# First attention of a two-layer fp32 step: two heads' scores inside the last query chunk, the query sums in two parts, one rope on GpSimd

## What is computed

```python
qa, ka, va, qi, ki, wi, cqlat, ckv, kr = split_cols(u @ w_in, AB_SPLITS)
q  = rope(rmsnorm(qa.reshape(nb, t, 8, 128), g_aq), pos)          # mixer A: 8 heads
...
qb = (rmsnorm(cqlat, g_qlat) @ w_uq).reshape(nb, t, 8, 128 + 64)  # mixer B
qn = rmsnorm(qb[..., :128], g_qn)
qr = rope(rmsnorm(qb[..., 128:], g_qr), pos)
...
# mixer A: scores, a mask from an index (top-k), softmax, values
s = einsum('bqcgd,bqscd->bqcgs', qg, k_sel) * 128 ** -0.5
p = softmax(where(valid, s, -inf)); o = einsum('bqcgs,bqscd->bqcgd', p, v_sel)
# mixer B: the same with nope and rope parts and other keys
```

## Time and profile before

| | |
|---|---|
| time, median of 3 runs | 2862.4 us (2862.0 to 2863.89) |
| the profiled execution | 2863.7 us, its span 2861.7 us |
| PE busy | 99% of the span, DVE 50%, ACT 37%, POOL 7% |
| the chain that ended last | PE 97%, DVE 2%, ACT 1% |
| the first attention with its query chunks | about 241 to 317 us of the span |
| mean granted TensorE clock | 0.999 of 2.4 GHz |

### The profile page before, as it was taken

One profiled execution on the slowest core, in us unless ns is written; L12 is line 12 of the kernel. 1 busy time (PEld: TensorE's weight loads), 2 busy tenths in 40 slices (PEclk: granted clock), 3 DMA queues, 4 the chain that ended last, 5 costly groups with the idle time before them and its releaser, 6 DMA issues.

```text
span 2861.7 us, 45023 instructions
## 1 busy us (share of the span) xinstructions
PE 2843.7 (99%) x18666; PEld 2798.6 (98%) x18666; DVE 1428.0 (50%) x1546; ACT 1069.6 (37%) x1236; POOL 186.0 (7%) x112
## 2 busy tenths in 40 slices
PE   9999999999999999999999999999999999999999
PEld 9997799999999999999999999899999999999999
DVE  7677645543443344344466774546444443444443
ACT  5334533332332333233335633434333332432332
POOL 2000002000000000000221241112000000000000
PEclk9999999999999999999999999999999999999999
DMA  6433024444444444444444444244444444444443
GB/s 232 139 114 111 30 89 143 144 140 145 143 140 148 140 145 142 141 146 140 145 149 155 154 146 148 97 160 149 148 152 151 148 152 149 148 152 149 149 153 135
DMA packets 112783, 405.25 MB, mean 142 GB/s; under 512 B 12656, under 2 KB 14752, under 8 KB 112480
## 3 DMA queue, kind: packets, MB, share of 16 engines
q1 hardware_dynamic: 108864, 392.64, 41.2%
q0 software_dynamic: 1616, 6.31, 0.6%
q10 hardware_dynamic: 2128, 3.66, 0.3%
HBM read 396.48 MB, written 6.09 MB: 141 GB/s over the span
## 4 chain that ended last, share of the span: by engine, by line
PE 97%; DVE 2%; ACT 1%; issue 0%; DMA 0%; ACTq 0%; DVEq 0%
PE PS L1426 31%; PE PS L1430 30%; PE PS L1431 30%; PE PS L1505 0%; ACT pr L498 0%; DVE pr L925 0%; DVE w_lo L858 0%; PE PS L1706 0%; DVE rb L1067 0%; PE PS L1503 0%; PE PS L1881 0%; PE PS L1489 0%; ACT w_hi L450 0%; PE PS L1753 0%; PE PS L1752 0%
## 5 line engine op out<-in xcount | busy, mean ns | idle before, releaser
L858 DVE TENSOR_TENSOR w_lo<-stage,w_hi 128x1024 fp32r<-128x1024 f32 x734 | 919.6, 1255 | 1192.6 <-ACT w_hi L450 1192.2
L450 ACT ACTIVATE w_hi<-stage 128x1024 fp32r<-128x1024 f32 x740 | 784.0, 1060 | 1628.2 <-PE PS L1431 1618.7
L1426 PE MATMUL PS<-xh,w_hi 128*128 128x336 f32 (+1 forms) x3264 | 1021.5, 313 | 1.1 <-DVE kk L1102 0.6
L1430 PE MATMUL PS<-xl,w_hi 128*128 128x336 f32 (+1 forms) x3248 | 1015.3, 313 | 0.0
L1431 PE MATMUL PS<-xh,w_lo 128*128 128x336 f32 (+1 forms) x3248 | 1014.6, 312 | 0.0
L1426 PE MATMUL PS<-hh,w_hi 128*128 128x336 f32 (+1 forms) x2032 | 635.2, 313 | 0.0
L1431 PE MATMUL PS<-hh,w_lo 128*128 128x336 f32 (+1 forms) x2032 | 635.1, 313 | 0.0
L1430 PE MATMUL PS<-hl,w_hi 128*128 128x336 f32 (+1 forms) x2032 | 634.9, 312 | 0.0
L1426 PEld LDWEIGHTS PS<-xh,w_hi 128*128 128x128 f32 x3264 | 614.4, 188 | 3.9 <-DVE w_hi L848 1.1
L1431 PEld LDWEIGHTS PS<-xh,w_lo 128*128 128x128 f32 x3248 | 612.1, 188 | 0.0
L1430 PEld LDWEIGHTS PS<-xl,w_hi 128*128 128x128 f32 x3248 | 611.5, 188 | 0.4
(11 more groups left out here) (343 smaller groups left out, 1527.7 us busy)
## 6 DMA issues: line engine op xcount, KB each, us to landing
stage<-in_wstream SPq DMA_DIRECT2D x740, 512.0 KB, 3.3
out_s<-so POOLq DMA_DIRECT2D x8, 256.0 KB, 2.6
x<-in_x_in SPq DMA_DIRECT2D x6, 336.0 KB, 7.2
out_y<-x ACTq DMA_DIRECT2D x3, 672.0 KB, 4.0
dmask<-in_ret POOLq DMA_DIRECT2D x4, 352.0 KB, 6.1
stage<-in_wstream SPq DMA_DIRECT2D x4, 256.0 KB, 3.6
s<-in_s_in POOLq DMA_DIRECT2D x1, 1024.0 KB, 5.3
x<-in_x_in SPq DMA_DIRECT2D x4, 168.0 KB, 3.7
```

The source lines that it names most:

```text
L450: act.activation(w_hi[s], halves_of(s), ACT.Copy).then_inc(hi_ready, 1)
L858: dve.tensor_tensor(w_lo[s], halves_of(s), w_hi[s].bitcast(F32), ALU.subtract).then_inc(lo_ready, 1)
L1426: pe.matmul(out, wh, rh, start=first, stop=False)
L1430: pe.matmul(out, wh, rl, start=False, stop=False)
```

## The change

Five edits, all between the last chunks of the query projection and the end of the first attention:

- The scores of heads 0 and 1 move from the head of `attend` into the last query chunk on PE (before its first and before its second unit), with their minima on DVE (`minima`) and their exponentials on ACT (`exponentials`). They use banks 2, 3 and 0, 1. `attend` begins at step 2, and its banks alternate the other way round.
- `query_sums` is split. The four matmuls of the rope parts (`pair_sums`) run after the first unit of the second chunk, into bank 2; the eight others run at step 3, not 1, into bank 7. Each part has its own DVE copy to `sdq`.
- The rope of mixer B's queries goes from DVE to POOL: five `tensor_tensor` instructions over 1344 elements per partition, with a new tile `rbq` in the place of `rb4`, begun when `pair_sums` is done (the tile lies where the squares were).
- `latl`, `gqk`, the memset of `ptb` and the norm of head 0 are placed between the minima of heads 0 and 1 and the last copy of the queries on DVE.
- The split of unit `U_KN` + 3 (the second value unit) moves behind the first attention on ACT and DVE.

```diff
+TURNS = 5
+        rbq = place("rbq", [P, 4, T], A + 28 * TB)
 # ACT
             for k in range(6):
-                split(U_UQ + 4 + k)
+                if k < 5:
+                    split(U_UQ + 4 + k)
                 ab_piece(7, 4 + k)
+                if k >= 4:
+                    exponentials(k - 4)
...
-            attend(0, 0, 0)
+            attend(0, 0, 0, 2)
+            split(U_KN + 3)
             split(U_KN + 4)
 # DVE
+            def minima(g, h, bias, scale, b0):
+                dve.wait_ge(sc_psum, g + 1)
+                if g >= 3:
+                    dve.wait_ge(pt_psum, g - 2)
+                ...                       # the three reductions that stood in attend
+            def normed(g):
+                ...                       # reciprocal and three products, as in attend
-                    if g0 == 0 and s == 1:
-                        dve.wait_ge(qb_ms, 1)
-                        dve.tensor_copy(sdq[0:8], PS[0:8, 4:6, 0:T]).then_inc(qb_taken, 1)
+                    if g0 == 0 and s == 3:
+                        dve.wait_ge(qb_ms, 2)
+                        dve.tensor_copy(sdq[0:8, 0], PS[0:8, 7, 0:T]).then_inc(qb_taken, 1)
...
-                if (g, j) == (7, 7):
-                    dve.wait_ge(qa_turned, 2)
-                    half_sines(rb4, qr, 2, 0, "qr")
-                    half_sines(rb4, qr, 2, 1, "qr")
-                if (g, j) == (7, 8): ...  # product with gain and cosines
-                if (g, j) == (7, 9): ...  # sum, qb_turned
...
             for k in range(6):
+                if k == 4:
+                    dve.wait_ge(bias_ready, 1)
+                    dve.wait_ge(qa_rinv, 2)
+                    minima(0, 0, biasA, scale_a, 2)
+                    dve.wait_ge(lath_ready, 2)
+                    dve.tensor_tensor(latl[:], lat[:], lath[:].bitcast(F32), ALU.subtract).then_inc(latl_ready, 1)
+                    dve.tensor_tensor(gqk[:], gcol("qn"), gcol("kn"), ALU.mult).then_inc(gqk_ready, 1)
+                    minima(1, 1, biasA, scale_a, 0)
+                if k == 5:
+                    dve.memset(ptb[0:NS_TOK, :, 80:T], 0.0)
+                    normed(0)
                 if k % 2: ...             # the copy of a query chunk, as before
-                split(U_UQ + 4 + k)
+                if k < 5:
+                    split(U_UQ + 4 + k)
+                if k == 2:
+                    dve.wait_ge(qb_ms, 1)
+                    dve.tensor_copy(sdq[0:8, 1], PS[0:8, 2, 0:T]).then_inc(qb_taken, 1)
                 ab_piece(7, 4 + k)
-                if k == 3: ...            # latl
-            ...                           # gqk, waits, memset
-            attend(0, 0, biasA, lambda h, q: ..., 0)
+            attend(0, 0, biasA, scale_a, 0, 2)
+            split(U_KN + 3)
+            dve.wait_ge(qb_turned, TURNS)
 # PE
             for c in range(3):
+                if c == 2:
+                    pe.wait_ge(qa_turned, 2)
+                    pe.wait_ge(qb_taken, 1)
+                    head_scores(0, scores_a, 2)
                 if c:
                     pe.wait_ge(qkv_evac, c)
                 for k in range(2):
+                    if (c, k) == (2, 1):
+                        pe.wait_ge(qa_rinv, 2)
+                        head_scores(1, scores_a, 0)
                     ...                   # the unit
+                    if (c, k) == (1, 0):
+                        pair_sums()
                     ab_side(7)(2 * c + k)
 # POOL, after its four output DMAs
+            pool.wait_ge(qkv_evac, 1)
+            pool.wait_ge(qb_ms, 1)
+            gain4 = gcol("qr").unsqueeze(1).to_broadcast([P, 4, T])
+            pool.tensor_tensor(qr, qr, gain4, ALU.mult).then_inc(qb_turned, 1)
+            pool.wait_ge(qb_turned, 1)
+            for a, b in ((slice(0, 64), slice(64, P)), (slice(64, P), slice(0, 64))):
+                sines = tab[a, 3, :].unsqueeze(1).to_broadcast([64, 4, T])
+                pool.tensor_tensor(rbq[b], qr[a], sines, ALU.mult).then_inc(qb_turned, 1)
+            pool.wait_ge(qb_turned, 3)
+            pool.tensor_tensor(qr, qr, cos4, ALU.mult).then_inc(qb_turned, 1)
+            pool.wait_ge(qb_turned, 4)
+            pool.tensor_tensor(qr, qr, rbq[:], ALU.add).then_inc(qb_turned, 1)
```

More of the change, by code:

```diff
@@ L486, in rms, with exponentials, attend @@
                 return f
-            def attend(g0, h0, sb):
+            def exponentials(g):
+                act.wait_ge(smax, g + 1)
+                for q in range(3):
+                    seg = pr[:, g % 3, SEG[q]:SEG[q + 1]]
+                    e = act.activation(seg, seg, ACT.Exp, scale=-1.0, bias=mx[:, g % 3, q:q + 1],
+                                       accum_out=rsum[:, g % 3, q:q + 1])
+                e.then_inc(p_ready, 1)
+            def attend(g0, h0, sb, s0=0):
                 pb, ob = 4 - sb, 6 - sb
-                for s in range(8 + 3):
+                for s in range(s0, 8 + 3):
                     if s < 8:
[L494 to L500, removed]
+                        exponentials(g0 + s)
                     if 2 <= s < 10:
@@ L915, in attend @@
+            def normed(g):
+                dve.wait_ge(p_ready, g + 1)
+                ch.link(dve.reciprocal(rsum[:, g % 3, :], rsum[:, g % 3, :]))
+                for q in range(3):
+                    seg = pr[:, g % 3, SEG[q]:SEG[q + 1]]
+                    e = dve.tensor_scalar(seg, seg, rsum[:, g % 3, q:q + 1], None, ALU.mult)
+                e.then_inc(pn_ready, 1)
+            def attend(g0, h0, bias, scale, sb, s0=0):
                 pb, ob = 4 - sb, 6 - sb
-                for s in range(8 + 3):
+                for s in range(s0, 8 + 3):
@@ L917, in attend @@
                     if s < 8:
                         g = g0 + s
[L919 to L927, removed]
@@ L928, in attend @@
-                        e.then_inc(smax, 1)
-                    if 1 <= s < 9:
[L930 to L936, removed]
@@ L1460, in sum_squares, with head_scores, attend @@
                 return f
-            def attend(g0, scores, values, sb, tail):
+            def head_scores(h, scores, b0):
+                for q, (t0, k0, k1) in enumerate(QT):
+                    o = SEG[q] - SEG[2] * (q // 2)
+                    mm = scores(h, PS[:, b0 + q // 2, o:o + k1 - k0], t0, k0, k1)
+                mm.then_inc(sc_psum, 1)
+            def attend(g0, scores, values, sb, tail, s0=0):
                 pb, ob = 4 - sb, 6 - sb
-                for s in range(8 + 3):
+                for s in range(s0, 8 + 3):
                     if s < 8:
@@ L1468, in attend @@
                             pe.wait_ge(smax, g - 1)
[L1469 to L1473, removed]
+                        head_scores(s, scores, (2 * ((g + 1) % 2) if g0 == 0 else sb + 2 * (g % 2)))
+                    if g0 == 0 and s == 3:
                         query_sums()
@@ L1478, in attend @@
                         if g == 0:
-                            pe.wait_ge(qb_taken, 1)
+                            pe.wait_ge(qkv_evac, 3)
                         if g == 8:
@@ L1500, in attend @@
                             pe.wait_ge(mol_ready, g - 1)
+                        if g == 1:
+                            pe.wait_ge(qb_taken, 2)
                         out = PS[:, ob + g % 2, 0:T]
@@ L1638, in _, with scores_a, pair_sums, query_sums @@
                     chunk(U_ABIN + CU * g, g, xh, xl, hook=ab_side(g))
+            def scores_a(h, out, t0, k0, k1):
+                return pe.matmul(out, zt[:, QA + h, t0:t0 + P], kA[:, h // 4, k0:k1], start=True, stop=True)
+            def pair_sums():
+                pe.wait_ge(qb_sq, 1)
+                for j in range(4):
+                    c = GAIN["selpair"] + 14 - 2 * j
+                    mm = pe.matmul(PS[0:8, 2, 0:T], gains[:, c:c + 8], sqq[:, 8 + j, :], start=j == 0, stop=j == 3)
+                mm.then_inc(qb_ms, 1)
+            def query_sums():
+                pe.wait_ge(qkv_evac, 3)
+                pe.wait_ge(qb_sq, 3)
+                for j in range(8):
+                    mm = pe.matmul(PS[0:8, 7, 0:T], sel("sel128", j), sqq[:, j, :], start=j == 0, stop=j == 7)
+                mm.then_inc(qb_ms, 1)
             pe.wait_ge(latl_ready, 1)
```

40 lines of the change are left out of this document (17 added, 23 removed).

## The result

| | median | runs | profiled execution, its span |
|---|---|---|---|
| before, on the same chip | 2863.26 us | 2861.87 to 2868.2, 10 runs | 2863.7, 2861.7 us (the profile shown above) |
| after | 2870.85 us | 2869.89 to 2871.29, 10 runs | 2871.13, 2869.0 us |

The ratio is 1.0027, with a 95% interval from 1.0018 to 1.0035: slower by 5 to 10 us, 7.6 us by the medians. The forecast was 6.7 us slower.

The account below looks back on a forecast made before the run. PE, holding 97% of the chain that ended last, was taken as the bound. Lateness at head 4 of 5.0 us plus 1.7 us of clock made 6.7, on 2862.4 a median of 2869.1 us, range 2859.5 to 2872.1.

Parts of the forecast that it names:

- The bound and the mark: PE holds 97% of the chain; the minimum of head 4, at 287.45 us before, shifts 5.0 us, everything behind keeping its distance.
- The hold-ups: DVE instructions before the last query copy wait for POOL's rope in five places, 11.8 us, against 6.3 us of rope gone.
- The fifth: Mixer A's rope sum on DVE, ready at 258.4, held behind POOL's gain product until 261.0: 2.6 us.
- the list: Forecast schedule of DVE and POOL turns from pair sums at 255.4 us to the query copy at 282.2.
- POOL's durations: Five rope products or sums over 1344 elements on POOL, 3.03 us each by length, 15.2 in all.
- PE's wait: After head 2's scores end at 276.0 us, PE waits 6.2 us for DVE's query copy.
- The order behind it: PE rows from head 0's transposes at 282.2 us through head 4's scores, putting head 4's minimum at 292.4.
- The clock: One fall of the granted clock to 0.50 behind PE's 6.2 us wait, half of 3.4: 1.7 us, ends 0 and 3.4.
- The sum: 5.0 us at head 4's minimum plus 1.7 us of clock: 6.7 us slower, median 2869.1 us.
- No hold-up: Rival: DVE instructions pass POOL freely or are held only now and then, 2.9 us faster, 2859.5 us; chance 0.15.
- The clock stays up: Rival: hold-ups come but no clock fall behind PE's wait, 5.0 us slower, 2867.4 us; chance 0.17.
- Small ones slip through: Rival: token scales and `gqk` find the port free between POOL instructions, 2.8 us slower, 2865.2 us; chance 0.14.

Follow-up runs that it names:

- e7: Kernel before with only the rope of mixer B's queries moved to POOL, scores, query sums and splits in the old order: 2868.99 us.
- e9: Changed kernel with twenty-four unused identity matmuls on PE in front of head 2's scores: 2866.5 us.
- e6: Changed kernel with sixteen unused identity matmuls on PE in front of head 2's scores: 2868.82 us.
- e1: Changed kernel without POOL's five instructions, the rope of mixer B's queries left out altogether: 2860.0 us.
- e8: Changed kernel with POOL's five products begun only when the minima of head 2 are done, in the first attention: 2865.89 us.
- e2: Changed kernel with 13 chained POOL memsets of the rope tile in place of the five products, rope left out: 2861.75 us.
- e4: Changed kernel with eighteen unused matmuls on PE behind a wait for head 1's minima, in front of head 0's transposes: 2869.08 us.

## Why the prediction was right, step by step

- *The bound and the mark.* PE's chain is the bound after as before, and behind the minimum of head 4 nothing more was lost or won: 7.35 us at head 4 and 7.35 us 120 us later. So the moved split of `U_KN` + 3 cost nothing, as forecast.
- *The hold-ups.* Four of the five came, close to their sizes: the split 1.9 us (forecast 1.5), the token scales 2.5 (2.7), `latl` 1.7 (2.0), `gqk` 2.9 (3.0). The fifth did not: L1199, the old L1185, took 1.54 us, no hold-up where I had 2.6. By the rows POOL's gain product starts ahead of it, at 258.77 against 259.08, and yet it was POOL that waited: 4.14 us, and 4.14 less 1.54 leaves 2.6 for the product itself. In e7, where POOL was well into its sines, the same sum was held. The miss cost nothing in the sum, because POOL waits once for that rope sum in either order: in the forecast behind its gain product, here in front of it. Its sines start at 262.26 (262.99 less the 0.73 of the start), against 262.5 in the list, and it is POOL's end that releases `gqk`.
- *POOL's durations.* 3.03 us each fits the cosines (3.04) and, with DVE's turns taken off, the sum (3.84 less 0.9) and the two sines (7.05 less some 1.0 for the split); the product with one gain per partition takes 2.42 us when it is alone (e7). The query copy ended 0.8 us earlier than forecast (282.16 less the 0.73 of the start is 281.4, against 282.2). About 0.2 of that is there when the sines start, and 0.7 when POOL ends (277.07 less 0.73 is 276.3, against 277.0), so most of it gathers in the turns behind the gain product.
- *PE's wait.* 4.48 us in place of 6.2: by 0.8 us because the copy was earlier, the rest because head 2's scores ended later than the 276.0 of the list, as the clock was at its lower level from 270.2 to 273.7. Late work in front of a wait costs nothing, so this fall is free.
- *The order behind it* (transposes, scores of head 3, query sums, values, scores of head 4) was right row for row.
- *The clock.* The mechanism was right and the size too small: 1.7 us forecast, 2.4 measured (e9 against after). I had one fall of 3.4 us with half of it lost. It lasted from about 280.5 to 287.3 us, twice as long, but the first 1.8 us of it lay in PE's wait. Where the fall lasted 3.4 us, as forecast, it cost 1.6 us (e6 against e9). Why it lasted twice as long after stays open. 2.4 is inside the ends of 0 and 3.4.
- *The sum.* 5.0 and 1.7 us were forecast, 4.2 and 2.4 came: 6.7 against 6.62 by the mark. Two misses of 0.8 and 0.7 us with opposite signs; that the sum agrees to 0.1 us is luck, that each term lies inside its ends is not. The medians are 7.6 us apart; the mark explains 6.6 of it, and what the last microsecond is stays open. The fall near 1820 us, which some executions have and others have not, makes 1.5 us between the profiles of after and e9, which is of that size, but no run shows that it is this. The forecast median of 2869.1 us was 1.75 too low: 0.9 of that is the difference, 7.6 in place of 6.7, and 0.9 the median of before, 2862.4 us in three runs and 2863.26 in ten.
- *The rivals.* Their prices can be read off the runs. "No hold-up" was 2859.5; e1, which leaves the rope out, gives 2860.0. "The clock stays up" was 2867.4, e9 gives 2866.5. "Small ones slip through" is excluded by the token scales and `gqk`, which were held for 2.5 and 2.9 us.

## What to carry to other kernels

Work given to GpSimd is not free beside VectorE if it reads SBUF: count what stands on VectorE in its span, with a hold-up of the rest of the running GpSimd instruction (once, in the kernel before, of two in a row) for each that has two SBUF inputs or is a product from SBUF to SBUF, however short (`gqk`, one element, was held for 2.9 us), while those that read PSUM passed here. Look first where VectorE waits anyway: 6.3 us of its own work cost 0.3 us in such gaps, the same rope on an idle engine cost 10. A wait of PE costs more than its length where the clock falls behind it, and a row of unused matmuls in front of the wait gave that part back where it left 0.76 us of it (e9), not where it left 2.55 us (e6).

## What was not expected of the hardware

- Which engine goes first is not read off the starts of the rows: POOL's row began 0.31 us before DVE's, and DVE's ran at its full speed while POOL's was 1.5 us longer.
- The reciprocal of 3 elements, SBUF to SBUF, is not held (0.17 us beside POOL's sines in e8), while the `tensor_scalar` product of 24 elements is, even by a memset (0.91 us in e2).
- A product by one value per partition takes POOL 2.42 us for 1344 elements (e7), one by 336 values per partition, used four times over, 3.04 (after).
- The clock fell behind pauses of PE of 1.95 us (after), 2.0 us (e4) and 2.55 us (e6), but in e4, e6 and e9 it did not behind the same pause of 1.94 us for the token scales; a wait of this length may cost the clock or not.
